# A hybrid decoder block with routed experts on one core: an expert item of at most 64 tokens puts high and low parts of its rows side by side in one stationary operand

## The reference, cut to what matters

```python
def expert_block(args):
    tok, g, e = args
    xb = h_pad[tok]                                   # rows of the normed input, D = 1024
    gu = xb @ w_gate_up[e] + b_gate_up[e]             # 1024 x 2048
    gate, up = jnp.split(gu, 2, axis=-1)
    gate = jnp.minimum(gate, SWIGLU_LIMIT)
    up = jnp.clip(up, -SWIGLU_LIMIT, SWIGLU_LIMIT)
    act = (up + 1.0) * (gate * jax.nn.sigmoid(SWIGLU_ALPHA * gate))
    y = act @ w_down[e] + b_down[e]                   # 1024 x 1024
    return y * g[:, None].astype(y.dtype)
```

## Time and profile before

| | |
|---|---|
| median of 3 runs | 2495.05 us (2492.78 to 2496.61) |
| profiled execution | 2494.33 us, span of the trace 2492.7 us |
| PE busy | 2278.7 us (91%), weight loads 1877.3 us |
| DVE busy | 1642.1 us (66%) |
| ACT busy | 1276.2 us (51%) |
| GpSimd busy | 333.0 us (13%) |
| DMA | 540.85 MB, mean 217 GB/s |

### The profile page before, as it was taken

The page is one execution under the profiler, slowest core; times in us unless marked ns, Lnnn a source line. Parts: engine busy times, 40 slices in busy tenths (PEclk is TensorE's granted clock), DMA queues, the critical chain, the costliest instruction groups (busy, mean ns, idle before and its releaser), DMA issues.

```text
span 2492.7 us, 35661 instructions
## 1 busy us (share of the span) xinstructions
PE 2278.7 (91%) x11202; PEld 1877.3 (75%) x11203; DVE 1642.1 (66%) x1730; ACT 1276.2 (51%) x1424; POOL 333.0 (13%) x305
## 2 busy tenths in 40 slices
PE   6999878797599999999999999999999999999991
PEld 5889645697487887877787777778888777888781
DVE  4311357555567669689869999966666997656772
ACT  5111257533345457467547777644444765445462
POOL 1000000012211102012102121211110221111110
PEclk8999969998699999999999999999999999999996
DMA  5111200333568669599869999976665997666844
GB/s 187 45 51 51 85 1 1 127 95 105 177 229 284 194 226 375 184 340 367 296 219 372 352 348 364 360 254 205 215 195 194 369 357 269 207 206 213 277 134 152
DMA packets 266914, 540.85 MB, mean 217 GB/s; under 512 B 14802, under 2 KB 31468, under 8 KB 266868
## 3 DMA queue, kind: packets, MB, share of 16 engines
q1 hardware_dynamic: 248884, 487.94, 55.5%
q0 software_dynamic: 17984, 52.29, 8.9%
HBM read 501.07 MB, written 39.11 MB: 217 GB/s over the span
## 4 chain that ended last, share of the span: by engine, by line
PE 55%; DVE 15%; issue 11%; ACT 3%; DMA 1%; ACTq 1%; DVEq 0%; POOL 0%; SPq 0%; POOLq 0%
PE ps L645 52%; DVE w_lo L1465 2%; DVE slots_between L1465 2%; DVE last_slot L1465 2%; ACT hT_hi L1098 2%; DVE region_mem L1498 1%; DVE work L1492 1%; DVE work L1503 1%; DVE work L1321 1%; PE ps L863 1%; PE ps L785 1%; PE ps L870 1%; DVE mem_there L1470 1%; DVE hT_lo L1476 1%; ACT hT_lo L1126 0%
## 5 line engine op out<-in xcount | busy, mean ns | idle before, releaser
L645 PE MATMUL ps<-hT_hi,hT_lo 128*128 128x512 f32 (+1 forms) x4736 | 1502.4, 388 | 12.6 <-DVE hT_lo L1484 12.6
L645 PEld LDWEIGHTS ps<-hT_hi,hT_lo 128*128 128x128 f32 x4736 | 886.2, 188 | 199.0 <-DVE w_lo L1465 18.5
L1098 ACT ACTIVATE hT_hi<-weight_ring 128x2048 fp32r<-128x2048 f32 x417 | 788.9, 1915 | 311.4 <-PE ps L645 269.6
L1465 DVE TENSOR_TENSOR slots_between<-weight_ring,hT_hi 128x2048 fp32r<-128x2048 f32 x245 | 554.1, 2288 | 118.6 <-ACT hT_hi L1098 114.4
L645 PE MATMUL ps<-slots_between,hT_lo 128*128 128x512 f32 x1344 | 524.4, 390 | 0.0
L1465 DVE TENSOR_TENSOR w_lo<-weight_ring,hT_hi 128x2048 fp32r<-128x2048 f32 x140 | 319.7, 2284 | 31.2 <-ACT hT_hi L1098 31.2
L645 PE MATMUL ps<-w_lo,hT_lo 128*128 128x512 f32 (+1 forms) x896 | 335.9, 375 | 0.0
L645 PEld LDWEIGHTS ps<-slots_between,hT_lo 128*128 128x128 f32 x1344 | 252.6, 188 | 53.6
L1120 ACT ACTIVATE region_mem<-work 128x512 f32<-128x512 f32 x96 | 57.2, 621 | 271.1 <-DVE work L1492 271.1
L645 PEld LDWEIGHTS ps<-w_lo,hT_lo 128*128 128x128 f32 x896 | 168.7, 188 | 30.3
L563 POOL DMA_INDIRECT residual_rows<-work,idx_now x48 | 118.8, 2475 | 477.3 <-ACT work L1137 402.3
(11 more groups left out here) (242 smaller groups left out, 2402.9 us busy)
## 6 DMA issues: line engine op xcount, KB each, us to landing
weight_ring<-in_w_gate_up SPq DMA_DIRECT2D x280, 1024.0 KB, 8.0
weight_ring<-in_w_down SPq DMA_DIRECT2D x140, 1024.0 KB, 5.7
weight_ring<-in_w_mix_in SPq DMA_DIRECT2D x10, 1024.0 KB, 5.6
weight_ring<-in_x SPq DMA_DIRECT2D x8, 512.0 KB, 8.9
weight_ring<-in_w_mix_out SPq DMA_DIRECT2D x4, 1024.0 KB, 4.9
work<-in_x SPq DMA_DIRECT2D x8, 512.0 KB, 5.2
residual_rows<-work SPq DMA_DIRECT2D x8, 512.0 KB, 3.7
normed_rows<-work SPq DMA_DIRECT2D x8, 512.0 KB, 5.0
```

Of the source, the lines that this page charges most:

```text
L645: return pe.matmul(o, l, r, start=first, stop=last)
L1098: act.activation(w_high_part(u), ring[:, home(u), :], ACT.Copy).then_inc(s["w_high_made"], 1)
L1465: dve.tensor_tensor(w_low_part(u), ring[:, home(u), :], w_high_part(u).bitcast(f32), ALU.subtract)\
```

## The change

Items are now of three kinds: `("full", "full")`, `("full",)` and `("short",)`, the last for one block of at most 64 tokens (SHORT). Each engine has a copy of the round's code for each kind. In a short item:

- The stationary operand, 128 columns, holds the high part of 64 rows in columns 0 to 63 and the low part in columns 64 to 127. `x_high`, `x_low`, `a_high` and `a_low` handle 64 columns per slice.
- PE makes two products per slice: this operand x weights high and x weights low. PSUM partitions 0 to 63 then hold high x (high + low), partitions 64 to 127 low x (high + low). For the bias `pick` gets a second form with ones only in the first 64 columns.
- The two halves are added afterwards: ACT copies partitions 64 to 127 to SBUF (`gate_rest`, `up_rest`, and `results` without scale), DVE adds partitions 0 to 63 (`add_rest`) and goes on in SBUF. There are six such pairs per item. The two of the output and the scaling by the gate weight are at the end of DVE's `item`.
- Gather and scatter move 64 rows.

Operations of DVE between SBUF operands use 64 partitions. In all other items the work stays, with one more semaphore increment at the end of ACT's and DVE's round.

```diff
+SHORT = P // 2
...
-        pick = ctx.enter_context(nc.sbuf_tensor("pick", [P, 4, P], f32r))
+        pick = ctx.enter_context(nc.sbuf_tensor("pick", [P, 4, P + SHORT], f32r))
...
+        def by_size(eng, size, body):
+
+            with eng.If(size > P + 1):
+                body(("full", "full"))
+            with eng.Else():
+                with eng.If(size > SHORT + 1):
+                    body(("full",))
+                with eng.Else():
+                    body(("short",))
...
+        def rows_of(kind):
+            return slice(0, P if kind == "full" else SHORT)
...
-                        mm(bank, pick[:, pick_row, :], pair_d if side == "d" else pair_gu, True, False)
+                        picked = pick[:, pick_row, 0:P] if kind == "full" else pick[:, pick_row, SHORT:SHORT + P]
+                        mm(bank, picked, pair_d if side == "d" else pair_gu, True, False)
                     for kk in range(4):
                         k = 4 * half + kk
-                        x_hi, x_lo = rows[:, k, b, 0, :], rows[:, k, b, 1, :]
-                        mm(bank, x_hi, high[:, kk, :], False, False)
-                        mm(bank, x_hi, low[:, kk, :], False, False)
-                        last = mm(bank, x_lo, high[:, kk, :], False, k == KD - 1)
+                        first, second = rows[:, k, b, 0, :], rows[:, k, b, 1, :]
+                        mm(bank, first, high[:, kk, :], False, False)
+                        last = mm(bank, first, low[:, kk, :], False, kind == "short" and k == KD - 1)
+                        if kind == "full":
+                            last = mm(bank, second, high[:, kk, :], False, k == KD - 1)
...
+            def gate_rest(it, c, kinds):
+                if "short" in kinds:
+                    b = kinds.index("short")
+                    act.wait_ge(s["w_used"], it * 12 + (HI_SLOTS + 4 * c + 2))
+                    act.wait_ge(s["a_made"], it * 2 + (c + 1))
+                    act.activation(gate_b[0:SHORT, b, :], ps[SHORT:P, out_bank("g", c, b), :], ACT.Copy).then_inc(s["rest_made"], 1)
...
+                    if kind == "full":
+                        ins = act.activation(y_rows[:, b, cols], ps[:, out_bank("d", c, b), :], ACT.Copy, scale=idx_now[:, b, 1:2])
+                    else:
+                        ins = act.activation(y_rows[0:SHORT, b, cols], ps[SHORT:P, out_bank("d", c, b), :], ACT.Copy)
+                ins.then_inc(s["rest_made"] if "short" in kinds else s["y_made"], 1)
...
                 high_unit(it, 4)
+                gate_rest(it, 0, kinds)
                 high_unit(it, 5)
-                sigmoids(it, 0, nb)
+                sigmoids(it, 0, kinds)
                 high_unit(it, 6)
+                up_rest(it, 0, kinds)
                 high_unit(it, 7)
-                sigmoids(it, 1, nb)
-                a_high(it, 0, nb)
+                gate_rest(it, 1, kinds)
+                sigmoids(it, 1, kinds)
+                a_high(it, 0, kinds)
                 high_unit(it, 8)
                 high_unit(it, 9)
+                up_rest(it, 1, kinds)
...
                 for c in range(2):
-                    results(it, c, nb)
+                    results(it, c, kinds)
+                if "short" not in kinds:
+                    act.sem_inc(s["rest_made"], 6)
...
+            def add_rest(it, n, place, bank):
+                dve.wait_ge(s["rest_made"], it * 6 + n)
+                dve.tensor_tensor(place, ps[0:SHORT, bank, :], place, ALU.add).then_inc(s["sum_made"], 1)
+
+            def gates(it, c, kinds):
                 dve.wait_ge(s["w_used"], it * 12 + (HI_SLOTS + 4 * c + 2))
                 dve.wait_ge(s["a_made"], it * 2 + (c + 1))
-                for b in range(nb):
-                    ins = dve.tensor_scalar(gate_b[:, b, :], ps[:, out_bank("g", c, b), :], LIMIT, None, ALU.min)
+                if "short" in kinds:
+                    b = kinds.index("short")
+                    add_rest(it, 2 * c + 1, gate_b[0:SHORT, b, :], out_bank("g", c, b))
+                for b, kind in enumerate(kinds):
+                    place = gate_b[rows_of(kind), b, :]
+                    if kind == "short":
+                        dve.wait_ge(s["sum_made"], it * 6 + (2 * c + 1))
+                    ins = dve.tensor_scalar(place, ps[:, out_bank("g", c, b), :] if kind == "full" else place, LIMIT, None, ALU.min)
...
+            def results(it, c, kinds):
+                if "short" in kinds:
+                    b = kinds.index("short")
+                    place = y_rows[0:SHORT, b, HALF * c:HALF * c + HALF]
+                    add_rest(it, 5 + c, place, out_bank("d", c, b))
+                    dve.wait_ge(s["sum_made"], it * 6 + (5 + c))
+                    dve.tensor_scalar(place, place, idx_now[0:SHORT, b, 1:2], None, ALU.mult).then_inc(s["y_made"], 1)
...
                     low_unit(it + 1, 1)
                     low_unit(it + 1, 2)
+                for c in range(2):
+                    results(it, c, kinds)
+                if "short" not in kinds:
+                    dve.sem_inc(s["sum_made"], 6)
                 dve.sem_inc(s["dve_item"], 1)
```

More of the change, by code:

```diff
@@ L351, in turn_bank, with by_first, by_second @@
             return 6 + b if c == 0 else 2 * b
+        def by_size(eng, size, body):
[6 more added lines that the diff above has]
+                    body(("short",))
+        def by_first(eng, size, body):
+            with eng.If(size > SHORT + 1):
+                body("full")
+            with eng.Else():
+                body("short")
+        def by_second(eng, size, body, without):
+            with eng.If(size > P + 1):
+                body("full")
+            with eng.Else():
+                without()
+        def rows_of(kind):
+            return slice(0, P if kind == "full" else SHORT)
         def out_bank(side, c, b):
@@ L948, in _ @@
                 with pe.If(size_now > 0):
[L949 to L952 removed]
+                    by_size(pe, size_now, lambda kinds: item(it, size_next, kinds))
                     pe.sem_inc(s["pe_item"], 1)
@@ L1175, in _ @@
             bias_gu_high(0)
-            for b in range(BLOCKS):
-                x_high(b, 0)
+            size_first = act.value_load(table[2:3, 1:2], min_val=0, max_val=CAP + 1)
+            by_first(act, size_first, lambda kind: x_high(0, 0, kind))
+            by_second(act, size_first, lambda kind: x_high(1, 0, kind), lambda: act.sem_inc(s_xhigh[1], 1))
             with act.Fori(0, MAX_ITEMS) as it:
@@ L1493, in gates, with products @@
                 ins.then_inc(s["gate_read"], 1)
-            def products(it, c, nb):
+            def products(it, c, kinds):
                 dve.wait_ge(s["sig_made"], it * 2 + (c + 1))
-                for b in range(nb):
-                    ins = dve.tensor_tensor(sig_b[:, b, :], gate_b[:, b, :], sig_b[:, b, :], ALU.mult)
+                for b, kind in enumerate(kinds):
+                    rows = rows_of(kind)
+                    ins = dve.tensor_tensor(sig_b[rows, b, :], gate_b[rows, b, :], sig_b[rows, b, :], ALU.mult)
@@ L1501, in products @@
                 dve.wait_ge(s["a_turned"], it * 2 + (c + 1))
-                for b in range(nb):
-                    ins = dve.tensor_scalar(up_b[:, b, :], ps[:, out_bank("u", c, b), :], LIMIT, -LIMIT, ALU.min, ALU.max)
+                if "short" in kinds:
+                    b = kinds.index("short")
+                    add_rest(it, 2 * c + 2, up_b[0:SHORT, b, :], out_bank("u", c, b))
+                for b, kind in enumerate(kinds):
+                    place = up_b[rows_of(kind), b, :]
+                    if kind == "short":
+                        dve.wait_ge(s["sum_made"], it * 6 + (2 * c + 2))
+                    ins = dve.tensor_scalar(place, ps[:, out_bank("u", c, b), :] if kind == "full" else place, LIMIT, -LIMIT,
+                                            ALU.min, ALU.max)
                 ins.then_inc(s["up_read"], 1)
@@ L1530, in item @@
                 low_unit(it, 10)
-                a_low(it, 1, nb)
+                a_low(it, 1, kinds)
                 low_unit(it, 11)
@@ L1548, in _ @@
             bias_low(0, pair_gu, raw_gu, s["bias_gu_high"], s["bias_gu_low"])
-            for b in range(BLOCKS):
-                x_low(b, 0)
+            size_first = dve.value_load(table[2:3, 1:2], min_val=0, max_val=CAP + 1)
+            by_first(dve, size_first, lambda kind: x_low(0, 0, kind))
+            by_second(dve, size_first, lambda kind: x_low(1, 0, kind), lambda: dve.sem_inc(s_xlow[1], 1))
             with dve.Fori(0, MAX_ITEMS) as it:
```

171 lines of the change are left out of this document (83 added, 88 removed).

## The result

| | before | after |
|---|---|---|
| median | 2495.32 us (2492.78 to 2496.61, 4 runs) | 2537.64 us (2537.33 to 2541.22, 4 runs) |
| span of the trace | 2492.7 us | 2535.7 us |

The changed kernel is slower: ratio of the mean times 1.0174, interval 1.0159 to 1.0189. That is 42.3 us between the medians, 43.0 between the spans. The forecast was 2530, so 35.7 more than before, with 2508 to 2546 as its range.

A forecast was written before the change was run, and what follows sets the result against it. DVE's instruction list, with a detour through ACT, was taken to bound one-block items. Items 16, 19, 27 (16.4 us), 4 and 7 (12.0), 32 (5.0) and full one-block items (2.3) add 35.7 to 2494.3: 2530 us, range 2508 to 2546.

The forecast's parts named there:

- Which items change, and who sets their pace: Six of 35 items (4, 7, 16, 19, 27, 32) turn short; DVE sets their pace, PE's 10.9 us become waits.
- The inner sums: DVE ahead of a_low(1): four gate and up sums at 0.72, four clamps 0.20 cheaper, +2.1 us per short item.
- The item's end: DVE behind low unit 2: two sums, two multiplications and the sequencer's uncovered loop round, +4.3 us, bounds 2.3 to 5.5.
- Narrower work: DVE and ACT on 256 columns: a_low and a_high -0.4 us; x_low -0.54, only for items 16, 19, 27.
- Item 32: Short item before a two-block one: PE waits 5.0 us for y_made at unit 0 of the next item's second block.
- Full one-block items: An added increment and branch at the end of ACT's round: 0.15 us in each of 16, +2.3, between 0 and 5.
- One sign of being wrong: The forecast counts as wrong if, among other signs, full one-block items no longer take 38.4 to 38.7 us.
- once only, ahead of the loop: Zeroing pick's second form and a table read on ACT and DVE, each under 0.5 us, left out of the sum.
- PE sets the pace: Rival for one-block items: each of six gives 10.9 us back, 2429 us; milder form 2478; together chance 0.06.
- Additions hidden: Rival: loop round stays covered and sums fall into DVE's waits for ACT, 0 to 5 us remain, 2497; chance 0.06.
- The clock falls: Rival: TensorE's clock drops in short items' pauses, 0 to 3 us an item, 2548 us at most; chance 0.13.
- The forecast's chain: DVE's instruction list, with its detour through ACT, gets longer and sets the time of one-block items; chance 0.75.

The follow-up runs named there:

- no_sums: Changed kernel with all six additions, ACT's copies for them and DVE's two output multiplications left out in short items; 2499.40 us, ratio 1.0017.
- third_product: Changed kernel with PE issuing a third product per slice again in short items, all additions kept; 2545.8 us, ratio 1.0203.
- results_early: Changed kernel with DVE's output sums and multiplications moved ahead of low unit 2 of the next item; 2526.27 us, ratio 1.013.
- copy_only: Changed kernel with the size test set so that no item is short: third code copy present, never run; 2506.61 us, ratio 1.0049.
- before_act_order: Kernel before the change, with ACT's a_high(0) and high unit 8 moved ahead of sigmoids(1); 2455.82 us, ratio 0.9846.
- no_inner_sums: Changed kernel without the four gate and up additions and ACT's copies for them in short items; 2526.11 us, ratio 1.0127.
- no_output_sums: Changed kernel without the two output additions in short items, ACT scaling the output as before; 2510.72 us, ratio 1.0066.

## Why the prediction came out as it did

**Which items change, and who sets their pace: right.** 288 bias products as before, and a short form in six items. PE's 48 products fewer were costed at nothing; `no_sums` (+0.1 us in six pairs) and `third_product` (40.22 and 40.23) show it from both sides. The picture drawn of it was off: PE is busy 33.2 us in item 16 and not under 30. Some of it is the lower clock (33.24 at 0.92, 31.79 at 0.96 in item 19).

**The inner sums, forecast +2.1: 1.9.** The forms, from the grouped view of DVE:

```profile
L1544 DVE TENSOR_TENSOR work<-ps,work 64x512 f32<-64x512 f32 x36 | 24.4, 677 | 0.2
...
L1556 DVE TENSOR_SCALAR work<-work 64x512 f32<-64x512 f32 x12 | 5.0, 420 | 0.4
...
L1591 DVE TENSOR_SCALAR work<-work,idx_now 64x512 f32<-64x512 f32 x12 | 5.7, 479 | 0.4
```

The sum was taken at 685 ns and has 677; the clamp at 0.49 and has 0.42, so it saves 0.26 and not 0.20 each. The rule of the Trainium skill that the prediction weighed (page "VectorE: DVE Perf Modes", section "The TRN2 errata") gives 0.33 us for this form; the trace differs, with 0.42 for constants and 0.48 for a scalar per partition. The row of 1024 columns was the nearer guide for the latter, and the clamp lies between the two.

**The item's end, forecast +4.3: 4.0 in the pair, 4.6 with the item behind it.** The mechanism was right: the sequencer's round, hidden before, comes out when the loop ends with a wait for DVE's own result. 2.60 us against 2.7 by ACT's row scaled with 190 to 152 ns. `results_early` takes it away with one low part as cover.

**Narrower work, -0.4 and for `x_low` -0.54: plausible, not measured by itself.** `no_sums` less `copy_only` is -0.5 us in the pairs 4+5 and 7+8 and -0.9 in 16+17, 19+20 and 27+28, where 0.4 and 0.94 had been taken. But `no_sums` also lacks an increment per round, and the item behind each pair is a further 0.6 to 0.9 us below `copy_only`, so these differences are no measurement of either term.

**Item 32, forecast 5.0 all as a wait for `y_made`: 5.2, by another way.** PE's order of time in item 33:

```profile
2370.37 0.49 PE L673 MATMUL ps<-mem_there,pick 128*128 128x512 f32 x1 [2.26 <-DVE hT_lo L1527]
...
2376.94 0.47 PE L673 MATMUL ps<-mem_there,pick 128*128 128x512 f32 x1 [1.75 <-DVE work L1591]
```

The second block waited first for the second `x_low`, 2.26 us, and only then, at its next bank, 1.75 for the last multiplication. The size was right because both hang on the same late list of DVE; the row named was only half of it.

**Full one-block items, forecast +0.15 each, +2.3 in all: too low.** The 3.5 us in "all other items" are those outside the pairs and items 1 and 2 alone, up to 0.5 each; the full items within the pairs come on top. `copy_only` has 2.9 in the pairs and 3.8 in the others, 6.7 in all. ACT's round got 0.37 longer, and in a run of one-block items (16 and 17 in `copy_only`) 0.36 of it shows in the time: the price was more than twice what was taken. One sign of being wrong was touched by it: full one-block items of the changed kernel reach 38.8, where 38.7 was the limit.

**A step that was wrong: "once only, ahead of the loop".** The prediction looked for costs that occur once and named `pick`'s second form and a table read. It left out the third copy of the code itself: 5.5 us in items 1 and 2. `copy_only`, in which the copy is never run, has 5.2 of them, and `third_product`, with 48 more products in it, a second one. That the wait is a load of instructions is likely: PE waits without a releaser, and every kernel with the third copy has one instruction packet more than the kernel before (31 against 30; `third_product` 34), while `before_act_order`, without the copy, has 30 and no such wait. No packet can be seen to end the wait, though. The Trainium skill, page "Advanced Engine Details and Errata", section "ISA Cache", gives TensorE 128 KB of instruction cache and the size of a line as 16 KB; the packets of the trace, 0.51 MB in 31, agree with that size, and code longer by one copy of the round would then need one line more. No run here shows how full it was, so this cause of the wait is argued and not shown.

**How near the sum came is partly luck.** `copy_only` parts the 42.3 us: 11.6 without any short item (forecast 2.3, so 9.3 too few) and 31.0 for the short form itself (forecast 33.4, so 2.4 too many). The two misses have opposite signs. 2530 was 7.6 too low, 1.0 of it because the sum started from 2494.3 and the time before is 2495.3 here. The range isn't the sum of the terms that stand beside it: 9 and 2.7 give 11.7 to either side, 2518 to 2542, not -22 and +14. That narrower range would have held the time as well.

**The rivals.** PE sets the pace (0.06): out, by two runs. Additions hidden (0.06): out, since `no_inner_sums` and `no_output_sums` add up to the whole. The clock falls (0.13, up to 3 us an item): it did fall, to a mean of 0.92 over item 16, so to the lower of its two levels (1.2 GHz in place of 2.4) for part of it, and it cost nothing: short items at 0.92 and 0.96 take the same 40.22 to 40.25, and 40.23 at 1.00 in `third_product`. The forecast's chain was right (0.75), and its range held the time because the misses offset each other, not because the one-time wait had been seen.

## What to carry to other kernels

Before work is taken off an engine, ask in the order of time who waits for whom: two engines busy for 36.7 and 35.7 of 38.4 us looked alike in the sums, and only the waits (PE 0.83 us for DVE, DVE 2.3 us for ACT) told that a third off PE is worth nothing and that swapping two steps of ACT is worth 39 us. A wait at the end of a loop's body uncovers the loop's own round (2.6 us on DVE here); put an independent operation behind it. A further copy of a large body of code can cost even where it is never run: count its branch and its increments in each round, and look once for a wait put down to issue at the first pass through the neighbouring body (here 5 us, probably a load of instructions).

## What the runs showed of the hardware that was not expected

- A copy of code that is never executed cost, with its branches and increments, 5.2 us once and 0.1 to 0.5 us in each one-block item. PE's waits without a releaser that came with it were 5.1 us, and 4.5 for the second in `third_product`; behind a full one-block item 0.22 us of ACT's round are the branch and 0.14 the increment.
- On DVE 64 partitions cost the same as 128: a sum of PSUM and SBUF with 512 columns took 677 ns with 64 and 685 with 128.
- The clamp of 512 columns read from SBUF took 420 ns with constants, 479 with a scalar per partition, and 687 when it read PSUM (there with 128 partitions).
- TensorE at a mean granted clock of 0.92 over a short item took 40.22 us, and at 0.96 over two others 40.25 and 40.23: the lower clock lost nothing where DVE set the pace.
